# Routed experts of 160 tokens: from gathered rows to a dense pass over all experts on the matrix engine

## What is computed

```python
q = (xb @ wq).reshape(blk, PEER_HEADS, 2, D_KEY // 2)
s1 = jnp.einsum('nhd,kd->nhk', q[:, :, 0], k1).astype(jnp.float32)
s2 = jnp.einsum('nhd,kd->nhk', q[:, :, 1], k2).astype(jnp.float32)
t1, i1 = lax.top_k(s1, TOPK_HALF)
t2, i2 = lax.top_k(s2, TOPK_HALF)
cand = (t1[..., :, None] + t2[..., None, :]).reshape(blk, PEER_HEADS, TOPK_HALF * TOPK_HALF)
ts, ti = lax.top_k(cand, TOPK)
e = (jnp.take_along_axis(i1, ti // TOPK_HALF, axis=-1) * N_KEYS
     + jnp.take_along_axis(i2, ti % TOPK_HALF, axis=-1))
g = jax.nn.softmax(ts, axis=-1)
hid = jax.nn.gelu(jnp.einsum('nd,nhkd->nhk', xb, eu[e]))
return jnp.einsum('nhk,nhkd->nd', (g * hid).astype(xb.dtype), ev[e])
```

## Time and profile before

| | us |
|---|---|
| time, median of 3 runs | 1820.68 |
| time, lowest and highest | 1814.56 and 1820.83 |
| the profiled execution: span from its first to its last instruction | 1820.2 |
| TensorE matmul busy in it | 1551.5 (85%) |
| VectorE busy | 1110.6 (61%) |
| GpSimd busy | 701.3 (39%) |
| ScalarE busy | 605.4 (33%) |

### The profile page before, as it was taken

How to read it: one execution, slowest core, us unless ns; L and a number is a source line. 1 busy time by engine, 2 the same in 40 slices (tenths; PEclk the granted TensorE clock), 3 DMA queues, 4 the chain that set the end, 5 groups by cost and what they waited for, 6 DMA issues and landing times.

```text
span 1820.2 us, 18420 instructions
## 1 busy us (share of the span) xinstructions
PE 1551.5 (85%) x5782; PEld 831.6 (46%) x5782; DVE 1110.6 (61%) x2783; ACT 605.4 (33%) x1873; POOL 701.3 (39%) x682
## 2 busy tenths in 40 slices
PE   8999997999888877788689999979888887877777
PEld 5779644554343332233147895545443333322221
DVE  3445766566888774444535367574868878654444
ACT  2332432333344332222333334323334423322222
POOL 5111343455544443334413024534464444434341
PEclk9999999999898899899999999989999988999999
DMA  9899999899999999999979989999999999999997
GB/s 334 319 386 355 410 412 421 365 421 422 420 421 421 422 421 422 421 423 420 422 295 396 379 355 407 420 374 416 421 422 420 422 421 422 421 421 421 421 423 309
DMA packets 102838, 730.03 MB, mean 401 GB/s; under 512 B 14993, under 2 KB 16114, under 8 KB 21972
## 3 DMA queue, kind: packets, MB, share of 16 engines
q0 software_dynamic: 90432, 627.75, 83.6%
q1 hardware_dynamic: 11760, 100.48, 13.9%
q10 hardware_dynamic: 548, 0.62, 0.1%
HBM read 724.54 MB, written 48.10 MB: 424 GB/s over the span
## 4 chain that ended last, share of the span: by engine, by line
PE 42%; DMA 41%; DVE 10%; ACT 3%; issue 2%; DVEq 1%; ACTq 1%; POOL 0%; SPq 0%
DMA arena<-peer_uv,idx 24%; PE bank L1762 22%; DMA wring<-peer_uv,idx 8%; PE bank L1518 7%; PE bank L1686 5%; DVE arena L1340 3%; DMA qf<-peer_uv,idx 3%; PE bank L1726 2%; DMA yt<-peer_uv,idx 2%; DMA wring<-w_out 2%; DMA arena<-peer_wq 2%; DVE wring L1340 1%; PE bank L1513 1%; ACT diag L864 1%; DVE yt L1340 1%
## 5 line engine op out<-in xcount | busy, mean ns | idle before, releaser
L1762 PE MATMUL bank<-arena,diag 128*128 128x512 f32 (+1 forms) x1416 | 679.2, 623 | 109.4 <-ACT diag L864 109.3
L1340 DVE SCALAR_TENSOR_TENSOR arena<-arena,xn 128x1024 f32<-128x1024 f32 x378 | 458.4, 1225 | 330.0 <-DMA arena<-peer_uv,idx 326.4
L641 POOL DMA_INDIRECT arena<-peer_uv,idx x378 | 410.0, 1085 | 617.9 <-PE bank L1762 462.8
L1762 PEld LDWEIGHTS bank<-arena,diag 128*128 128x128 f32 (+1 forms) x1416 | 265.3, 193 | 476.1 <-issue 298.5
L856 ACT ACTIVATE act<-hid 128x2 f32<-128x2 f32 x287 | 58.4, 204 | 903.4 <-DVE arena L1340 594.1
L864 ACT ACTIVATE diag<-ident,weight 128x128 f32<-128x128 f32 (+1 forms) x574 | 194.3, 385 | 20.9 <-issue 1.4
L1762 PE MATMUL bank<-wring,diag 128*128 128x512 f32 x336 | 165.2, 631 | 37.2 <-ACT diag L864 37.1
L641 POOL DMA_INDIRECT wring<-peer_uv,idx x84 | 98.8, 1176 | 129.0 <-PE bank L1762 119.9
L1762 PE MATMUL bank<-qf,diag 128*128 128x512 f32 (+1 forms) x216 | 111.3, 655 | 40.9 <-ACT diag L864 40.9
L1340 DVE SCALAR_TENSOR_TENSOR wring<-wring,xn 128x1024 f32<-128x1024 f32 x84 | 102.3, 1225 | 69.7 <-DMA wring<-peer_uv,idx 68.4
L859 ACT ACTIVATE weight<-act,gate 128x1 f32<-128x1 f32 x574 | 138.0, 287 | 19.8
(11 more groups left out here) (290 smaller groups left out, 1564.9 us busy)
## 6 DMA issues: line engine op xcount, KB each, us to landing
kvs<-cache_a_kv_w SPq DMA_DIRECT2D x32, 1022.0 KB, 10.7
wring<-w_col SPq DMA_DIRECT2D x15, 1024.0 KB, 8.1
wring<-w_tok SPq DMA_DIRECT2D x8, 1408.0 KB, 9.0
arena<-peer_wq SPq DMA_DIRECT2D x10, 1024.0 KB, 18.1
kvs<-cache_a_kv_w SPq DMA_DIRECT2D x16, 508.0 KB, 11.9
arena<-peer_uv,idx POOLq DMA_INDIRECT x378
qf<-cache_keys POOLq DMA_DIRECT2D x8, 576.0 KB, 10.7
qf<-cache_values POOLq DMA_DIRECT2D x8, 576.0 KB, 19.1
```

The costliest lines, as they stand in the source:

```text
L641: pool.indirect_dma_start(out=ring[j], out_offset=None, in_=io["peer_uv"], in_offset=bass.IndirectOffsetOnAxis(ap=idx[:, n:n + 1], axis=0) ...
L1340: last = v.scalar_tensor_tensor(out=ring[j][:, 0:D], in0=ring[j][:, 0:D], scalar=1.0, in1=xn[:, i, :], op0=ALU.mult, op1=ALU.mult, accum_o ...
L1762: last = pe.matmul(bank[b0 + half][0:r, :], diag[:, n % 16, 0:r], ring[SLOT_OF[n]][:, D + 512 * half:D + 512 * half + 512], start=False, s ...
```

## The change

Tile 0 keeps its gathers, but its weighted sum moves from TensorE to VectorE. The other 160 tokens no longer gather. All 16384 experts of the layer are streamed through TensorE for them, in blocks of 128 experts (512 KB each):

- `up`: 128 blocks of `u`, each a product with 8 steps of 128 x 128 weights and 160 columns; ScalarE applies gelu and keeps the result `hw` in SBUF.
- `gates`: for each token a 128 x 128 matrix of gates is built from its picks. ScalarE makes a one-hot matrix of the first key (`hots_a`, a Square and a Relu for each token), VectorE one of the second key for 8 tokens at once (`hots_b`), and TensorE multiplies them. VectorE multiplies `hw` with the result (`scale`). This goes in groups of 8 tokens, 20 groups for the first 64 blocks and 20 for the second.
- `down`: 128 blocks of `v`, 8 steps each, from `hw` into PSUM.

`u` and `v` are laid out by block ahead of the launch (`u_blocks`, `v_blocks`). SP streams them through 5 slots (`up`) and 7 slots (`down`). Tile 0 has a ring of 6 slots. VectorE works on it in pairs of columns: `dots(k)` and then `weigh(k-1)`, where `weigh` adds two columns to `yacc`. Tables of numbers tie the order on the engines together: `GATES_BEHIND` says behind which block a group of gates stands, `ACT_BEFORE` before which block's gelu the gelu of a pair stands, `PAIRS_GATES` how many pairs follow a group. The routing has nine parts, all of two heads; all queries stand before the first block. The next layer begins when both results are complete; nothing of it is interleaved any more. The last 36 of 168 cache copies of a layer now stand between the first `up` blocks, and loads of the next layer's first weights and keys between the `down` blocks.

The diff, cut to its core:

```diff
+U_SLOTS, V_SLOTS, RING = 5, 7, 6
+PARTS = ((0, 0, 2), (0, 2, 2), (0, 4, 2), (0, 6, 2), (1, 0, 2), (1, 2, 2), (1, 4, 2), (1, 6, 2), (2, 0, 2))
+SCORE_BEHIND = {3: 0, 4: 2, 5: 4, 6: 7, 7: 13, 8: 21}
+TURN_BEHIND = {1: 59, 2: 69}
+GATES_BEHIND = [72 + 57 * g // 20 for g in range(PASS)] + [1 + 31 * g // 10 for g in range(PASS)]
+PAIRS_PART = (0, 1, 1, 1, 1, 1, 1, 1, 1)
+PAIRS_GATES = [(g + 1) * 6 // 5 - g * 6 // 5 for g in range(PASS)] + [(g + 1) * 13 // 10 - g * 13 // 10 for g in range(PASS)]
...
+            def load_u(l, n):
+                s, _ = slot_loads(l, 0, n)
+                if n < U_SLOTS - 1:
+                    sp.wait_ge(qf_ps, NQ * l + q_count(1 + n // 2, 1, REST))
+                elif n < U_SLOTS:
+                    sp.wait_ge(qf_ps, NQ * l + 1)
+                else:
+                    sp.wait_ge(block_used, used(l, 0, n - U_SLOTS + 1))
+                sp.dma_start(slot[s], io["u_blocks"][l, n]).then_inc(block_in[s], 16)
...
+                for n in range(P):
+                    if n % 32 == 0:
+                        pool.wait_ge(idx_done, 4 * l + n // 32 + 1)
+                    if n >= RING:
+                        pool.wait_ge(v_used, P * l + n - RING + 1)
...
+                    pool.indirect_dma_start(
+                        out=ring[n % RING], out_offset=None, in_=io["peer_uv"],
+                        in_offset=bass.IndirectOffsetOnAxis(ap=idx[:, n:n + 1], axis=0)).then_inc(row_in[n % RING], 16)
...
+            def hots_a(l, g, tokens=range(TG)):
...
+                for t in tokens:
+                    a.activation(hot_a[g % 2][:, t, :], count[:, :], ACT.Square, bias=picks[:, 0, m0 + t:m0 + t + 1])
+                a.drain()
+                for t in tokens:
+                    last = a.activation(hot_a[g % 2][:, t, :], hot_a[g % 2][:, t, :], ACT.Relu,
+                                        bias=picks[:, 2, m0 + t:m0 + t + 1], scale=picks[:, 3, m0 + t:m0 + t + 1])
...
+            def weigh(l, k):
+                c = slice(2 * k, 2 * k + 2)
+                v.wait_ge(act_done, PAIRS * l + k + 1)
+                v.tensor_tensor(hid[:, c], hid[:, c], gate[:, c], ALU.mult)
+                for n in (2 * k, 2 * k + 1):
+                    v.drain()
+                    row = ring[n % RING][:, D:2 * D]
...
+                        last = v.scalar_tensor_tensor(out=yacc[:, :], in0=row, scalar=hid[:, n:n + 1], in1=yacc[:, :], op0=ALU.mult, op1=ALU.add)
+                    last.then_inc(v_used, 1)
...
+            def up(l, n):
...
+                for k in range(KCH):
+                    last = pe.matmul(bank[n % 3][:, 0:DENSE], slot[j][:, k * P:(k + 1) * P], xt[:, k, REST], start=(k == 0), stop=(k == KCH - 1))
+                last.then_inc(block_used, 1)
...
-            def add_rows(l, n, i, last_one):
-                b0, r = 4 + 2 * (i % 2), ROWS[i]
-                pe.wait_ge(diag_done, COLS * l + n + 1)
-                for half in range(2):
-                    last = pe.matmul(bank[b0 + half][0:r, :], diag[:, n % 16, 0:r], ring[SLOT_OF[n]][:, D + 512 * half:D + 512 * half + 512],
-                                     start=False, stop=last_one)
...
+                for n in range(NK):
+                    up(l, n)
+                    for p in range(NP):
+                        if SCORE_BEHIND.get(p) == n:
                             score(l, p)
+                    for i in TURN_BEHIND:
+                        if TURN_BEHIND[i] == n:
+                            turn_picks(l, i)
+                    for g in range(PASS):
+                        if GATES_BEHIND[g] == n:
+                            gates(l, g)
+                for n in range(NK):
+                    down(l, n)
+                    for g in range(PASS, 2 * PASS):
+                        if GATES_BEHIND[g] == n:
+                            gates(l, g)
+                turn_y(l)
```

More of the change, by code:

```diff
@@ L92 @@
-CUTS = ((FIRST, (0, KCH)), (REST, (0, 4, KCH)), (WHOLE, (0, 3, 6, KCH)))
-NQ = len(Q_ORDER)
[L96 to L101, removed]
+SAMPLES = slice(SEQ, TOKENS)
+Q_ORDER = [(c, j, FIRST) for c in range(4) for j in range(2)]
+Q_ORDER += [(c, j, REST) for c in range(4) for j in range(2)]
@@ L102 @@
+Q_ORDER += [(c, j, WHOLE) for c in range(4, 8) for j in range(2)]
+NQ = len(Q_ORDER)
 PITCH = 384
 LOW = -3.0e38
[L105 to L130, removed]
@@ new lines, in trunk @@
+        chosen = take(2 * COLS).rearrange("p (a n) -> p a n", a=2)
+        assert at <= ring_at
+        ring = [big[:, ring_at + 2 * D * j:ring_at + 2 * D * (j + 1)] for j in RING_ORDER]
+        flat_blocks = big[:, blocks_at:blocks_at + U_SLOTS * D]
+        hot = big[:, hot_at:hot_at + 3 * D]
+        flat_xt = xt[:, :, :].rearrange("p k n -> p (k n)")
+        slot = [flat_blocks[:, j * D:(j + 1) * D] for j in range(U_SLOTS)] + [flat_xt[:, j * D:(j + 1) * D] for j in range(V_SLOTS - U_SLOTS)]
@@ L1443, in _ @@
-                v.tensor_scalar(layer0[:, :], layer0[:, :], float(NE), None, ALU.add)
+                h_apply(l, 1)
+                k = 0
+                for p in range(NP):
+                    route_top(l, p)
+                    if p:
+                        route_gate(l, p - 1)
+                    route_merge(l, p)
+                    route_pick(l, p)
+                    for _ in range(PAIRS_PART[p]):
+                        pair(l, k)
+                        k += 1
+                route_gate(l, NP - 1)
@@ L1446, in _ @@
+                for g in range(2 * PASS):
+                    hots_b(l, g)
+                    if g:
+                        scale(l, g - 1)
+                    for _ in range(PAIRS_GATES[g]):
+                        pair(l, k)
+                        k += 1
+                scale(l, 2 * PASS - 1)
+                for k in range(k, PAIRS + 1):
+                    pair(l, k)
+                for n in range(ADDS):
+                    x_add(l, n)
         @block.tensor
@@ L1769, in add_sample_rows @@
[L1769 to L1777 removed]
+                            r = slice(NS * q, NS * q + NS)
@@ new lines, in down @@
+            def down(l, n):
+                j, target = slot_loads(l, 1, n)
+                if n == 0:
+                    pe.wait_ge(gelu_done, NK * (l + 1))
+                    pe.wait_ge(scaled, PASS * (2 * l + 1))
+                if n == HALF:
+                    pe.wait_ge(scaled, PASS * (2 * l + 2))
+                pe.wait_ge(block_in[j], target)
+                for k in range(KCH):
+                    end = k in (2, 5, KCH - 1)
+                    last = pe.matmul(acc_of(k), slot[j][:, k * P:(k + 1) * P], hw[:, n, :], start=(n == 0 and k % 3 == 0), stop=(n == NK - 1 and end))
+                    if n == NK - 1 and end:
+                        last.then_inc(y_ps, 1)
+                if n < NK - 1:
+                    last.then_inc(block_used, 1)
```

1231 lines of the change are left out of this document (551 added, 680 removed).

## The result

The changed kernel takes 2019.42 us (median of 4 runs, 2013.63 to 2022.62), the kernel before in the same comparison 1820.76. The ratio is 1.110, with a 95% interval of 1.107 to 1.113. The forecast was 1955 with a range of 1870 to 2075: the sign and the range hold, the forecast was 64 us short.

The account below looks back on a forecast made before the run. Expert blocks were taken as bound by bytes, mixers by TensorE; in the changed kernel TensorE decides A and D. Layer 0 sums to 986 us, layer 1 brings 1950, the end 8: 1958, stated as 1955, range 1870 to 2075.

Parts of the forecast that it names:

- heads: Start of each layer up to its first scores: 190 us in layer 0, 175 in layer 1; +26 and +46.
- A: Routing beside `up`, first scores to first gates: TensorE decides, 221 us a layer; transfer engines idle some 57 us.
- D: Rest of `down` after the last gates: TensorE decides, 67 blocks at 2.17 us, put at 150 us a layer.
- B: Gates beside `up`: 20 groups with 24 pairs at 8.3 us each, 199 us a layer.
- C: Gates beside `down`: 20 groups with 26 pairs at 8.3 us, 216 us a layer, plus 7 for weights in layer 0.
- the pair: Two gathered columns of tile 0 beside the gates: 8.3 us, between 7.95 (bytes) and 9.2 (ring of three pairs).
- my formula for the ring: In the stretches with gates, a pair takes at least (L + 5.1 + 2.2)/2 us, L from slot free to landed.
- The third of the bytes for blocks: Engines take packets from queues in turn, so 4 KB block rows get a third beside a gather: 8.3 a pair.
- Bytes decide: Rival: A's idle transfer time fills up and time follows bytes, 663 MB at 401 GB/s, 1653 us; chance 0.08.
- TensorE's pace everywhere: Rival: B and C run at 8.0 and 8.5 us a group, 160 + 170, no waits, 1765 us; chance 0.04.
- half hidden: Rival: heads or waits cheaper than worked out, 1810 to 1885 us; chance 0.05.
- GpSimd is held up: Rival: each indirect issue takes 1 us more beside VectorE, a pair 9.3 us, total 2055 us; chance 0.13.

Follow-up runs that it names:

- the light kernel: The changed kernel without cache copies and with only half of each streamed block loaded, all engine instructions kept: 1831.99 us, ratio 1.007.
- large copies: The changed kernel with cache copies as in the kernel before, 32 large pieces a layer in place of 168 of 128 KB: 1944.94 us, ratio 1.068.
- half blocks: The changed kernel loading only the first half of each streamed block (256 KB), all engine instructions kept: 1914.80 us.
- the best one tried: The changed kernel with large copies, 14 of 24 groups in the mixer, 10 behind up block 4; 13 pairs behind the gates, paced: 1882.44 us, ratio 1.034.

## Why the prediction was right, and where it was short

**Slower, for the reason given.** The work moved from the transfers to TensorE, and the stages bound by it (heads, queries, A, D) leave transfers idle. The strip shows the idle transfers, and the light kernel shows that bytes alone do not bring the time under that of before. The size was helped by luck: 106 us that the sum lacked in the heads, A and D met 52 that it had too many in B, C and the end.

**The heads: the step that failed.** "With 1.5 us for a late weight it starts at 190" took the mixer's copies to cost nothing. The change had recut them, and I counted their bytes (unchanged) but neither their issues nor their packets: 37 us a layer. With large copies the first scores stand at 190.4 and the second head is 177.2, against 190 and 175. The marks show the same shift: first gather 244.0 for "near 206" (207.5 with large copies), first block of `up` 281.4 for "near 245" (244.9).

**A**: 9 and 6 us over. TensorE's pace was right (167.4 from first block to first gates with half blocks, worked out as 166); full blocks come late, so the transfers were not simply idle there. Near 300 GB/s was right too: windows from the first scores to the first gates have 297 and 300.

**B and C**: the pair was put at 8.3 between bounds of 7.95 and 9.2. It measured 7.8 in B (187.6 / 24), 8.2 and 7.9 in C (7.9 in both without the 7 us for weights in layer 0). The lower bound, bytes, was the right one. B was a little under it: 24 pairs and 56 blocks are 79.7 MB, and the window of B moved 74.6, so the other 5 had been fetched ahead. Block loads and gathers both took 10.3 us to land in B (medians), a little more than the 6.9 to 9.9 worked out; by my formula for the ring that would be 8.8 us or more a pair, so not all of its terms add up. The third of the bytes for blocks while a gather flows is borne out by the packets of the trace: in those microseconds of B and C in which a gather and a block were both well under way (2.5 us past their issue, 1.5 us ahead of landing), blocks had 32 to 36% of the bytes; in B of layer 0 that was 4,566 packets of the gathers and 4,038 of the other queue.

**D**: 150 was TensorE's pace, which half blocks reach (147.7 and 149.8). The other 9 are blocks that arrive behind gathers. VectorE takes the last columns at once, and its last pair is long done when D ends; so the 145 us that needed only 48 MB did have a wait in them.

**The durations** held: gates 1.89 us a group for 1.8, additions 1.285 us in the mean for 1.23, `hots_b` and `scale` 0.68 each for 0.65 to 0.7, ScalarE's one-hots 0.36 us apiece for 0.35.

**Rivals.** *Bytes decide* and *TensorE's pace everywhere* are out by 250 us and more, though B and C do go by bytes; *half hidden* ended at 1885, 134 below. *GpSimd is held up* came half: issues are 1420 ns in the mean for 1085, and by pairs the first is held and the second is not:

```profile
511.87 1.93 POOL L962 DMA_INDIRECT big<-peer_uv,idx  x1 [4.33 <-DVE yacc L1336]
514.10 0.94 POOL L962 DMA_INDIRECT big<-peer_uv,idx  x1 [0.30 <-issue]
```

One us later for every second column, and the pair stays at 7.8 because bytes bound it. The held issue runs beside the second addition of `weigh` (L1336, 510.31 to 512.98), the quick one beside the end of `scale`. So it is throughout: 122 of the 256 issues begin beside L1336 and take 1.88 us in the mean, the 67 beside `scale` and the 34 beside an idle VectorE 0.94. The Trainium skill, "SBUF — State Buffer", section "SBUF: two separate sides", has an exclusive lock between VectorE with two SBUF inputs and a GpSimd instruction that reads SBUF. On the issues the trace agrees with it. On VectorE it shows no such wait: 83 dots begin while an issue runs and take 1.25 us in the mean, for 1.22 without one. The price of 9.3 a pair that I drew from the lock does not follow where the transfers are the limit.

## What to carry to other kernels

When a change recuts a background transfer, count its packets and what each carries, not only its bytes: here, from memory to memory, the same bytes occupied the transfer engines 1.6 to 1.9 times as long in 8 KB packets as in large ones. A design that lowers total bytes gains only where its stages leave no engine alone: lay the stages out, find the one that binds in each, and spread the transfers over those that another engine binds. Before polishing such a version, take its bytes away on trial; here that gave 1832 us, so no order of the transfers alone was likely to bring the change under the 1820 of before, though the best one tried won 137 us on the changed kernel.

## What the runs showed of the hardware that was not expected

- Copies from memory to memory, by the queue's share: 430 GB/s in packets of up to 64 KB, 222 to 265 in packets of 8 KB, at full transfer share. The median 8 KB packet is as quick as a large one for its bytes (0.31 us); a fifth to a third of them are not. The gathers, rows of 8 KB into SBUF, took 0.32 us a packet in the mean in the same traces. The weights did suffer beside the small copies: 0.54 us for a packet of 11 KB, 0.48 beside large ones.
- A copy whose outermost dimension is eight has eight small packets in place of sixteen, and weights beside it land late: 2032 us with 672 data packets of 65 KB, 1945 with 1,024 that are on average smaller.
- An indirect issue of GpSimd takes 0.94 us, and 1.88 when it begins beside an addition of `weigh` on VectorE; VectorE is hardly slower for it (1.25 us a dot for 1.22).
- Waits for weights and a lower clock of TensorE go together. Behind a gap of 5.13 us the same instruction takes 0.8 us five times, and 2 us later 0.46; the windows of the two stretches have a granted clock of 0.50 and 1.00 (third column from the end), that is 1.2 and 2.4 GHz; the mean granted clock of the mixers is 0.93 and 0.89, for 0.99 and 1.00 before:

```profile
80.55 0.80 PE L1502 MATMUL bank<-big,xt 128*32 128x352 f32 x1 [5.13 <-DMA big<-w_tok]
...
82.90 0.79 PE L1502 MATMUL bank<-big,xt 128*32 128x352 f32 x1
...
85.59 0.46 PE L1502 MATMUL bank<-big,xt 128*32 128x352 f32 x1
```

```profile
80.50:83.50 3.00, 2.95 (x34) 2.51 (x35) 0.00 (x0) 0.00 (x0) 0.00 (x0) 0.50 0.99 186
85.50:87.50 2.00, 2.00 (x50) 2.00 (x44) 0.00 (x0) 0.00 (x0) 0.00 (x0) 1.00 1.01 424
```
